# 32 of 384 dense tokens take their first expert layer from fetched rows, and VectorE makes the lower parts of the query weights

## The reference

```python
for each of 8 heads:
    s1 = q1 @ k1.T ; s2 = q2 @ k2.T            # q = x @ w_query, 128 keys on each side
    v1, i1 = top_k(s1, 16) ; v2, i2 = top_k(s2, 16)
    top, pos = top_k(v1[:, None] + v2[None, :], 16)
    eidx = i1 * 128 + i2, at pos               # 16 experts for each token and head
    g = softmax(top)
hid = u_tab[eidx] . x                          # first expert layer, 128 slots a token
a = g * gelu(hid)
out = sum over slots of a * v_tab[eidx]        # second expert layer
```

## Time and profile before

| | |
|---|---|
| median of 3 runs | 1698.84 us (1697.75 to 1703.23) |
| profiled execution, its own time | 1703.0 us |
| span of its trace | 1701.4 us |
| mean granted TensorE clock | 0.981 |
| TensorE matmuls busy | 1622.1 us, 95% of the span |
| VectorE busy | 1353.9 us, 80% |
| ScalarE, GpSimd busy | 777.5 us, 613.5 us |

### The profile page before, as it was taken

How to read it: one execution, slowest core, us unless ns; L and a number is a source line. 1 busy time by engine, 2 the same in 40 slices (tenths; PEclk the granted TensorE clock), 3 DMA queues, 4 the chain that set the end, 5 groups by cost and what they waited for, 6 DMA issues and landing times.

```text
span 1701.4 us, 27754 instructions
## 1 busy us (share of the span) xinstructions
PE 1622.1 (95%) x9666; PEld 1460.0 (86%) x9666; DVE 1353.9 (80%) x3162; ACT 777.5 (46%) x1273; POOL 613.5 (36%) x538
## 2 busy tenths in 40 slices
PE   5999988798999999989999999999999999999997
PEld 4999744497999999989999999997888888888886
DVE  4324585353799999979999999987999999999996
ACT  4222373233434433367777767753333333333334
POOL 0000380054444444654334334432343333433320
PEclk9999997997999999999999999999999999999999
DMA  3342562722343333499999999999999999999991
GB/s 119 106 164 92 167 190 91 264 89 77 114 148 109 122 114 109 156 364 375 384 372 393 387 367 393 400 405 388 404 403 399 404 404 399 405 403 399 402 366 53
DMA packets 158621, 463.54 MB, mean 272 GB/s; under 512 B 18224, under 2 KB 64432, under 8 KB 154546
## 3 DMA queue, kind: packets, MB, share of 16 engines
q1 hardware_dynamic: 98930, 248.59, 39.7%
q0 software_dynamic: 50944, 178.96, 27.6%
q10 hardware_dynamic: 8640, 34.61, 5.1%
HBM read 406.12 MB, written 57.63 MB: 273 GB/s over the span
## 4 chain that ended last, share of the span: by engine, by line
PE 60%; DVE 13%; POOL 3%; DMA 2%; issue 1%; ACT 1%; another core or an unknown queue 0%; SPq 0%; ACTq 0%; POOLq 0%
PE va L230 10%; PE va L232 10%; PE va L231 10%; PE hp L230 6%; PE hp L231 6%; PE hp L232 6%; DVE gathered L1511 3%; DVE og L2039 3%; DVE ulo L2050 3%; PE ggp L1979 2%; DVE vw L1511 2%; PE qzp L230 2%; PE qzp L232 2%; PE qzp L231 2%; PE qsp L1680 1%
## 5 line engine op out<-in xcount | busy, mean ns | idle before, releaser
L230 PE MATMUL hp<-mid_hi,uhi 128*128 128x384 f32 x1024 | 354.0, 346 | 9.9 <-DVE ulo L2050 3.6
L231 PE MATMUL hp<-mid_lo,uhi 128*128 128x384 f32 x1024 | 344.8, 337 | 0.0
L232 PE MATMUL hp<-mid_hi,ulo 128*128 128x384 f32 x1024 | 343.5, 335 | 0.0
L230 PE MATMUL va<-vhi,ahi 128*128 128x512 f32 x768 | 299.8, 390 | 2.8 <-DVE hid L1511 2.1
L232 PE MATMUL va<-vhi,alo 128*128 128x512 f32 x768 | 299.5, 390 | 0.0
L231 PE MATMUL va<-vlo,ahi 128*128 128x512 f32 x768 | 299.3, 390 | 0.0
L1909 POOL DMA_INDIRECT gathered<-in_v_experts,eidx x160 | 175.6, 1098 | 310.3 <-DVE acc L2359 221.5
L230 PEld LDWEIGHTS hp<-mid_hi,uhi 128*128 128x128 f32 x1024 | 192.9, 188 | 15.0 <-DVE ulo L2050 5.8
L232 PEld LDWEIGHTS hp<-mid_hi,ulo 128*128 128x128 f32 x1024 | 193.0, 188 | 0.0
L231 PEld LDWEIGHTS hp<-mid_lo,uhi 128*128 128x128 f32 x1024 | 192.8, 188 | 0.0
L1420 ACT ACTIVATE uhi<-uw 128x1024 fp32r<-128x1024 f32 x126 | 132.8, 1054 | 116.1 <-PE hp L232 114.6
(11 more groups left out here) (328 smaller groups left out, 3448.6 us busy)
## 6 DMA issues: line engine op xcount, KB each, us to landing
uw<-in_u_experts SPq DMA_DIRECT2D x128, 512.0 KB
vw<-in_v_experts SPq DMA_DIRECT2D x68, 512.0 KB
more_v<-in_v_experts SPq DMA_DIRECT2D x60, 512.0 KB
gate_matrix<-gst ACTq DMA_DIRECT2D x12, 2048.0 KB
hidden_values<-gelu_out SPq DMA_DIRECT2D x72, 192.0 KB
hd_mid<-hidden_values SPq DMA_DIRECT2D x8, 1536.0 KB
gt_mid<-gate_matrix SPq DMA_DIRECT2D x8, 1536.0 KB
hd_freed<-hidden_values SPq DMA_DIRECT2D x7, 1536.0 KB
```

The costliest lines, as they stand in the source:

```text
L230: nc.tensor.matmul(out, a_hi, b_hi, start=first, stop=False)
L231: nc.tensor.matmul(out, a_hi, b_lo, start=False, stop=False)
L232: return nc.tensor.matmul(out, a_lo, b_hi, start=False, stop=last)
```

## The change

- The last 32 tokens of token tile 3 ("own" tokens) leave the dense first layer: each of its matmuls has 352 columns (`DENSE`) instead of 384, and so has each GELU.
- Their 32 x 128 slots become 32 gathers and 32 dots, four for each head (128 partitions hold 32 tokens times 4 slots). At the end of a head VectorE writes 32x16 expert numbers, SyncE spreads them with four small DMAs, GpSimd issues the four gathers two heads later between its tile subtractions, and VectorE does the four dots in the same head, behind links 10, 12, 14 and 16. The dots of the last two heads come behind the last head. The results are turned to GELU values, copied back and multiplied into the gates; the dense columns of the own tokens are set to 1.
- VectorE makes the lower parts of the query weights, behind links 1 and 11; GpSimd no longer does.
- VectorE makes the lower parts of tiles 42 and 43, between dots of the last two heads. GpSimd issues the last head's four gathers and five ordinary ones ahead of tile 44's lower part.
- Of the 160 old dots, 3 and 6 more are done ahead of the turns, then 6, and the turns hold 22, 21, 22, 21, 22 and 22 instead of 25, 20, 25, 20, 25 and 25.
- The loops over heads are written out on all five engines.

```diff
+OWN = 32
+DENSE = TD - OWN
+OWN_GROUPS = P // OWN
+OWN_SLOTS = TOPK // OWN_GROUPS
...
-                last = mm3(hp[i][:, :TD], uhi[:, i, k], ulo[:, i, k], x2hi[:, k, P:SEQ], x2lo[:, k, P:SEQ],
+                last = mm3(hp[i][:, :DENSE], uhi[:, i, k], ulo[:, i, k], x2hi[:, k, P:P + DENSE], x2lo[:, k, P:P + DENSE],
                            k == 0, k == KD - 1)
...
+        LENT = 10
+        EARLY = (5, 7, 8, 9, 9, 9)
+        OWN_LINKS = (10, 12, 14, 16)
+        FIRST_DOTS, BEFORE_TABLE, BEFORE_TURNS = 15, 3, 9
+        TURN_DOTS = (22, 21, 22, 21, 22, 22)
...
+            def own_spread(sp, j):
+                sp.wait_ge(own["picked"], j + 1)
...
+                for g in range(OWN_GROUPS):
+                    sp.dma_start(own_index[g * OWN:(g + 1) * OWN, j % 2], own_stage[mine, g * OWN_SLOTS:(g + 1) * OWN_SLOTS]).then_inc(own["index"], 16)
+
+            def own_fetch(pool, j, n):
+                if n == 0:
+                    pool.wait_ge(own["index"], 16 * OWN_GROUPS * (j + 1))
...
+            def own_dot(dve, j, n):
+                dve.wait_ge(own_row[j % 2], 16 * OWN_SLOTS * (j // 2 + 1))
...
             def route_on_gpsimd(pool):
...
                     for u in range(2):
                         u_split_lo(pool, RT * j + 2 + u, u, (2 + u) % UR)
-                        if not last:
-                            split(2 * j + 2 + u, u)
+                        if j >= 2:
+                            own_fetch(pool, j - 2, u)
...
+                for e in range(2, LENT):
+                    u_split_lo(pool, RT * NH + e, e % 2, e % UR)
+                    if e < 2 + OWN_SLOTS:
+                        own_fetch(pool, NH - 2, e - 2)
+                for n in range(OWN_SLOTS):
+                    own_fetch(pool, NH - 1, n)
+                for n in range(EARLY[0]):
+                    request(pool, n)
+                pool.wait_ge(u_lo, RT * NH + LENT + 1 + 3)
+                for i, e in enumerate(range(LENT + 2, QX + 1)):
+                    u_split_lo(pool, RT * NH + e, e % 2, e % UR)
+                    for n in range(EARLY[i], EARLY[i + 1]):
+                        request(pool, n)
...
             def route_on_vector(dve):
...
+                        if links[0] == 1 and j < NH - 1:
+                            split(2 * j + 3, 1)
+                        if links[0] == 11 and j < NH - 2:
+                            split(2 * j + 4, 0)
+                        if j >= 2 and links[0] in own_at:
+                            own_dot(dve, j - 2, own_at[links[0]])
                         dve.wait_ge(qs["chain"], j * LINKS + links[0])
...
+                dve.wait_ge(u_lo, RT * NH + LENT - 1 + 3)
+                for u in range(2):
+                    for n in range(u * OWN_SLOTS // 2, (u + 1) * OWN_SLOTS // 2):
+                        own_dot(dve, NH - 2, n)
+                    split_lo(dve, RT * NH + LENT + u, (LENT + u) % 2, (LENT + u) % UR)
+                for n in range(OWN_SLOTS):
+                    own_dot(dve, NH - 1, n)
                 dve.wait_ge(table_spread, 16 * SG)
                 nc.vector.tensor_copy(eidx[:, :, SG:], spread_idx[:]).then_inc(gs["tab"], 1)
```

More of the change, by code:

```diff
@@ L1555, in route_on_sync @@
                 sp.dma_start(slot_sum[:], A["slot_sum"]).then_inc(x2r_spread, 16)
-                with sp.Fori(0, NH - 1) as j:
+                for j in range(NH - 1):
                     for u in range(2):
@@ new lines, in route_on_sync @@
+                    if e == LENT:
+                        own_spread(sp, NH - 1)
+                    if e == LENT + 1:
+                        sp.wait_ge(table_prep, 2)
+                        for g in range(SG):
+                            cols = slice(g * SR, (g + 1) * SR)
+                            sp.dma_start(spread_idx[NS * g:NS * (g + 1), :, 0], sample_idx[:, cols]).then_inc(table_spread, 16)
+                    if e == QX:
+                        sp.wait_ge(own["act"], 1)
+                        for g in range(OWN_GROUPS):
+                            sp.dma_start(own_act[mine, :, g * OWN_SLOTS:(g + 1) * OWN_SLOTS], own_hid[g * OWN:(g + 1) * OWN]).then_inc(own["back"], 16)
@@ L1634, in route_on_scalar @@
                 act.sem_inc(qs["hi"], 2)
[L1635 to L1637 removed]
+                for j in range(NH):
+                    turn(j, j == NH - 1)
+                    if j == 0:
+                        act.wait_ge(own["x2"], 16 * OWN_GROUPS)
+                        act.wait_ge(fs["split_lo"], 2 * TT)
+                        nc.scalar.activation(x2own[:], gb[:, 0], ACT.Copy).then_inc(own["copied"], 1)
                 for e in range(QX):
@@ L1698, in route_on_tensor @@
                     hidden_product(pe, i, i % 2)
-                with pe.Fori(1, NH) as j:
+                for j in range(1, NH):
                     for u in range(2):
@@ L1723, in route_on_vector, with split @@
                 LINKS = 18
+                def split(n, u):
+                    dve.wait_ge(qs["hi"], n + 1)
+                    nc.vector.tensor_tensor(wlo[:, u], w[:, u], whi[:, u].bitcast(F32), ALU.subtract).then_inc(qs["lo"], 1)
+                split(2, 0)
                 ut = [(u, t) for u in range(2) for t in range(TT)]
-                with dve.Fori(0, NH) as j:
+                own_at = {link: n for n, link in enumerate(OWN_LINKS)}
+                for j in range(NH):
                     links = [0]
@@ L2000, in turn @@
                 j = 2 * pair + half
-                first = FIRST_DOTS + (pair * PAIR_ROWS + half * ROW) * ROW
-                n = (ROW if last else TURN_ROWS[half]) * ROW
+                first, n = FIRST_DOTS + sum(TURN_DOTS[:j]), TURN_DOTS[j]
                 at = 0
@@ L2040, in build_one_hots @@
                 last.then_inc(gs["oh"], 1)
-            def dot(n):
-                row, b = divmod(n, ROW)
-                dve.wait_ge(gathered[n % LOOK], 16 * (n // LOOK + 1))
-                multiply(dve, n % LOOK, b, hid[:, row, b:b + 1])
-            def split_lo(m, i, r):
-                dve.wait_ge(u_hi, m + 1)
-                nc.vector.tensor_tensor(ulo[:, i], uw[:, r], uhi[:, i].bitcast(F32), ALU.subtract).then_inc(u_lo, 1)
             def turn(pair, half, last):
                 j = 2 * pair + half
-                first = FIRST_DOTS + (pair * PAIR_ROWS + half * ROW) * ROW
-                rows_here = ROW if last else TURN_ROWS[half]
+                first, here = FIRST_DOTS + sum(TURN_DOTS[:j]), TURN_DOTS[j]
                 at, built = 0, AHEAD
@@ L2063, in turn @@
                         built += 1
-                    split_lo(G0 + GTI * j + i + 2, i % 2, slot(half, i + 2))
-                    while at < rows_here * ROW * (i + 1) // GTI:
-                        dot(first + at)
+                    split_lo(dve, G0 + GTI * j + i + 2, i % 2, slot(half, i + 2))
+                    while at < here * (i + 1) // GTI:
+                        dot(dve, first + at)
                         at += 1
-            dve.wait_ge(gs["x2p"], 2)
+            for n in range(BEFORE_TABLE, BEFORE_TURNS):
+                dot(dve, n)
             dve.wait_ge(u_lo, G0 + 3)
-            split_lo(G0 + 1, 1, 1)
+            split_lo(dve, G0 + 1, 1, 1)
             for i in range(AHEAD):
                 build_one_hots(0, i)
-            for n in range(FIRST_DOTS):
-                dot(n)
+            for n in range(BEFORE_TURNS, FIRST_DOTS):
+                dot(dve, n)
             over_turns(dve, turn)
```

127 lines of the change are left out of this document (84 added, 43 removed).

## The result

| | before | after |
|---|---|---|
| median | 1699.9 us (4 runs) | 1758.13 us (4 runs, 1757.33 to 1761.1) |
| ratio, 95% interval | | 1.0344 [1.0322, 1.0366] |
| span of the trace | 1701.4 us | 1756.8 us |
| mean granted clock | 0.981 | 0.963 |

Slower, as forecast, but by 58 us where 30 were forecast, and outside the range. The spans differ by 55.4. Busy time by stretch of the changed kernel; columns as in the earlier trace rows: VectorE's eight heads, from their end to turn 0, turn 0, turns 1 to 5, the last eight tiles.

The account below looks back on a forecast made before the run. VectorE's head chain, lengthened by GpSimd collisions, and the gather chain behind it set turn 0: +44.6 there, -2.3 turn 0, -11.5 turns 1 to 5, -1 last tiles, +29.8 on 1698.84 gives 1729 us, range 1709 to 1751.

Parts of the forecast that it names:

- heads end (collisions 15, 30.0 us): VectorE's last head ends at 735.2 us: start 431.6, clean heads 236.0, inserts 37.6, collisions with GpSimd subtractions 30.0.
- gather chain and seam to turn 0: Behind VectorE's last head: index, spreading, four gathers, landing, dots, tiles 44 and 45, slow clock; 42.4 us to turn 0.
- last eight tiles: After the turns: 36.7 us before; fewer columns save 2.6 at most, loads queue behind others, so -1 us.
- I take 15: VectorE's eight heads: 15 collisions with GpSimd subtractions, 30.0 us; bounds 0 and the 23 (46 us) of the kernel before.
- clean head: A VectorE head without collisions with GpSimd subtractions, put at 29.5 us; eight take 236.0.
- insert: Subtraction or dot put into VectorE's heads: 14 subtractions and 24 dots, 38 at 0.99 us, 37.6 us in all.
- slower still: Rival, chance 0.22: in VectorE's heads collisions stay at 23 (1745 us), or moved subtractions collide as well (1755 us).
- the landing of the last own gather: In the gather chain behind the last head: taken as 5.5 us after its start, between 1.4 and 8.8.
- Three dots fewer, one more ahead of it: -2.3: Turn 0, 70.7 us before with VectorE behind, gets 2.3 us shorter through its changed number of dots.
- VectorE becomes the bound: Turns 1 to 5: VectorE needs 308.3 us, TensorE 302.2; with half the gaps kept 311.9 instead of 323.4, -11.5.
- columns that save nothing: Rival: a matmul has a fixed price, so the turns give back little; 1741 us, chance within the 0.22 for slower.
- The sum had 3.4 us for it: TensorE, after waiting over 5 us for tile 44, runs at the 1.2 GHz level for 3.4 us, costing 1.7.

Follow-up runs that it names:

- e13: The changed kernel without GpSimd's 32 lower-part subtractions of the expert tiles in the heads (stale lower parts used): ratio 1.0131, span 1717.3 us.
- e3: The changed kernel without the gathers, dots and spreading DMAs of the 32 own tokens: ratio 1.0134 to the kernel before, span 1720.8 us.
- e12: The changed kernel with all its gathers and waits but without the 32 dots of the own tokens: ratio 1.0207, span 1731.8 us.
- e11: The changed kernel without the last head's four gathers, its dots kept on rows of an earlier head: ratio 1.0245, span 1741.6 us.
- e6: The whole changed kernel with lower parts, gathers and loads reordered around turn 0's start, own tokens' GELU two tiles later: ratio 1.0317, span 1754.2 us.
- e7: The changed kernel with four GELU output buffers instead of two in the six turns: ratio 1.0256, span 1744.5 us.
- e1: The kernel before with only the 352 columns in the first layer's matmuls and GELUs: ratio 0.9997, span 1697.6 us.
- e2: The kernel before with the query weights' lower parts on VectorE and its loop over heads written out: ratio 1.0029, span 1705.2 us.

## Why the prediction was wrong in size

The direction and the main mechanism were right: VectorE's chain and the gather chain behind it set turn 0. But each stretch was priced too low, 25.5 us in all, and behind the heads two waits had no term, for the returned activations and for the GELU stores:

| step of the prediction | predicted | measured | miss |
|---|---|---|---|
| heads end (collisions 15, 30.0 us) | 735.2 | 741.5 | +6.3 |
| gather chain and seam to turn 0 | 42.4 | 46.7 | +4.3 |
| turn 0 | 68.4 | 75.2 | +6.8 |
| turns 1 to 5 | 311.9 | 319.0 | +7.1 |
| last eight tiles | 35.7 | 36.7 | +1.0 |

**Heads.** The step that failed is "I take 15" collisions: there were 24, with 42.3 us instead of 30.0, +12.3. The other terms held. By e13 a clean head is 29.6 and an insert 0.90 instead of 0.99, and there are 37 inserts in the heads, not 38 (the first subtraction ends before them): 8 x 29.6 + 37 x 0.90 + 42.3 = 312.4, against 312.5 measured. The inserts give back 4.3, the clean heads take 0.8, and a first head at 429.0 instead of 431.6 gives another 2.6. The share of GpSimd's subtractions that hit rose from 25 of 55 to 24 of 38. The rival "slower still" named it: collisions stay, and moved subtractions collide as well (four of the 13 in the heads did). Its other reason, that every insert lengthens the stretch in which a hit can fall, has e3 and e12 against it: without the 24 dots there were 24 hits as well. The Trainium skill (SBUF — State Buffer, "Who interferes with whom") says it by kinds: VectorE's instructions with two SBUF inputs, and `copy`, `cast` and `tensor_scalar` in their two-port modes, share a port pair with GpSimd, and the whole instruction blocks. The trace agrees: all lengthened ones are of these kinds, never MAX8 or its companions. It agrees for the dots too. Their second input lies in PSUM (`x2own`, `x2p`), so that only one is in SBUF, and the twelve that ran beside a GpSimd subtraction in the changed kernel took 1.21 to 1.31 us, such as this one (start, length). So of the inserts the 13 subtractions could be hit and the 24 dots could not; GpSimd's relief was worth counting only against the former.

```profile
781.02 2.41 POOL L1429 TENSOR_TENSOR ulo<-uw,uhi 128x1024 fp32r<-128x1024 f32 x1 [0.36 <-ACT uhi L1425]
782.21 1.22 DVE L1520 CUSTOM_DVE_ANT_0 vw<-vw,x2p 128x1024 f32<-128x1024 f32 x1
```

**Gather chain.** The order of the links was right. The term that failed is the landing of the last own gather: taken as 5.5 between 1.4 and 8.8, it was 9.9. Two issues took 0.9 more each, and the spread indices 0.6; in all +6.8 at tile 44, of which 2.5 come back before turn 0. 5.5 was the price of a gather by itself: in the heads, such ones landed 4.2 to 5.5 us after their start, while the last head's four, started within 5.6 us, took 6.4, 8.9, 9.9 and 9.8. Behind them GpSimd started four ordinary gathers at once, and SyncE five loads; how much of it is theirs stays open.

**Turn 0.** "Three dots fewer, one more ahead of it: -2.3" was the wrong count. Ten more ordinary dots stand ahead of turn 0 and three fewer in it. They were taken as lying in TensorE's wait, but VectorE has gaps there of its own, and turn 0 ends with VectorE. From the end of the heads to turn 1 it is 121.9 us instead of 85.4, and VectorE's list accounts for it: eight own dots, two lower parts and, in the traces, 35 ordinary dots instead of 27, 18 x 1.14 = 20.5; 13.4 more in gaps over half a microsecond (25.4 instead of 12.0); and a softmax product (L1924) that took 3.65 instead of 0.82, with tile 44's lower part on GpSimd beside it (3.65 in e11 and e12 as well, 0.82 in e3 and e6). Among the gaps are the 11.0 above, 4.5 for the returned activations, which had no term in the sum, and 4.2 at the start of turn 0 for ordinary gathers.

**Turns.** VectorE's work was right to 0.2 us (308.45), TensorE was not the bound, and the bytes permitted it. The step that failed is "VectorE becomes the bound": what was put at nothing is a resource between the engines, two GELU buffers with stores that land a median of 7.8 us after issue and up to 14.5 in the chain. The earlier trace rows shows a DMA share of 1.00, and I read it only as bytes. Before, TensorE's 322.0 us hid that delay. e7 removes it and gives 307.8, less than the forecast's 311.9.

The rival "slower still" had the heads right (23 collisions or more, some of them on moved subtractions) and gave 1745 to 1755; measured were 1758, since it too left out the misses behind the heads. The rival beside it, columns that save nothing, is refuted for TensorE (its matmuls start 0.16 us apart, below, which makes 3.9 us a tile instead of 4.17) and nearly held for the time: TensorE is busy 12.4 us less in turns 1 to 5, and that, with seven fewer dots on VectorE, bought 4.4. The misses of all five rows have one sign, and nothing cancelled; that the direction came out right is not luck, since the forecast's own reasons for it (the inserts, the gather chain) are what e11, e12 and e3 price at 36 of the 55 us.

## What to carry to other kernels

Draw up the time line of the engine that binds, gaps included, across stages; here VectorE's runs from the first head to the end of turn 5, and the change added 37 inserts, ten operations behind them and a landing to it while it relieved TensorE. Where a saving uncovers an engine, ask which buffers and landings have lain under the old bound: here, at a DMA share of 1.00, late stores cost 11 us at 380 GB/s, and with two more buffers 394 GB/s went through. The collisions here did not scale with the other engine's instruction count (55 to 38 subtractions, 25 to 24 hits); take them away in one run and read the clean time, and see whether anything waits for it, since 28 us of them were worth 2.6 before the change.

## What the runs showed that I had not expected

- A column edit on TensorE alone moved GpSimd's subtractions against VectorE's chain and made 30 collisions of 25, +5.9 us in the heads (e1).
- The written-out loops over heads have no run of their own; e2 suggests 0.4 us a head for VectorE's.
- An indirect gather's issue (0.94 us by itself) that began while VectorE's lower-part subtraction ran ended about 2.03 us after that subtraction's start: begun 0.16 us into it, it took 1.87, 0.58 into it 1.46, 0.89 into it 1.14. 2.03 less 0.94 is 1.09, about the 1.14 us after which VectorE's next instruction starts, so it looks as if the issue waits for the subtraction to be done. Issues begun a quarter of a microsecond or more ahead of the subtraction mostly took 0.94. Beside a dot, with its one input in SBUF, they never took more than 0.97 (70 of them); the one at 747.48, beside the dot at 747.42, took 0.94.
- After the gap of 13.5 us TensorE's tile 44 ran with matmuls 0.29 us apart for 4.8 us at a granted clock of 0.51, which is the 1.2 GHz level, and then 0.16 apart at 1.00. The sum had 3.4 us for it. Two neighbours of either stretch (start, length):

```profile
773.39 0.49 PE L235 MATMUL hp<-mid_hi,uhi 128*128 128x352 f32 x1
773.69 0.49 PE L236 MATMUL hp<-mid_lo,uhi 128*128 128x352 f32 x1
...
774.83 0.32 PE L235 MATMUL hp<-mid_hi,uhi 128*128 128x352 f32 x1
774.99 0.32 PE L236 MATMUL hp<-mid_lo,uhi 128*128 128x352 f32 x1
```
